# FFN down products of a two-layer trunk: 18 of 22 inner tiles in Strassen blocks, low parts made by VectorE

## The reference

```python
D_MODEL = 1024
D_FF = 2816
def swiglu(h, w_gu, w_down):
    g, u = jnp.split(h @ w_gu, 2, axis=-1)
    return (jax.nn.silu(g) * u) @ w_down
# x = x + gate * swiglu(modulate(rmsnorm(x), ...), w_gu, w_down)
```

## Time and profile before

| | us |
|---|---|
| runs | 2856.87, 2859.77, 2854.50 (median 2856.87) |
| profiled execution | 2856.11, of it span 2854.2 |
| TensorE, VectorE, ScalarE, GpSimd busy | 2752.9, 1492.7, 935.1, 1160.0 |
| mean granted clock of TensorE | 0.988 of 2.4 GHz |

### The profile page before, as it was taken

One profiled execution on the slowest core, in us unless ns is written; L12 is line 12 of the kernel. 1 busy time (PEld: TensorE's weight loads), 2 busy tenths in 40 slices (PEclk: granted clock), 3 DMA queues, 4 the chain that ended last, 5 costly groups with the idle time before them and its releaser, 6 DMA issues.

```text
span 2854.2 us, 61199 instructions
## 1 busy us (share of the span) xinstructions
PE 2752.9 (96%) x22137; PEld 2550.0 (89%) x22137; DVE 1492.7 (52%) x2891; ACT 935.1 (33%) x2091; POOL 1160.0 (41%) x1256
## 2 busy tenths in 40 slices
PE   6999999999999999999889999999999999999999
PEld 5898999998999999999787787878789999998998
DVE  4767678665333343423556666666676434335224
ACT  5121212355433443000543233332464444440004
POOL 4000000355555564333754333333376666653324
PEclk8999999999999999999999999999999999999999
DMA  7422111544555535631133524343453333246422
GB/s 260 135 75 92 51 39 38 196 132 135 190 195 191 186 103 196 222 113 43 56 114 102 159 86 148 97 136 109 151 181 117 112 95 118 89 131 244 150 67 82
DMA packets 335403, 366.41 MB, mean 128 GB/s; under 512 B 25188, under 2 KB 272087, under 8 KB 333799
## 3 DMA queue, kind: packets, MB, share of 16 engines
q1 hardware_dynamic: 311282, 327.13, 35.0%
q10 hardware_dynamic: 15732, 28.31, 2.8%
q0 software_dynamic: 8192, 8.40, 1.1%
HBM read 281.95 MB, written 81.82 MB: 127 GB/s over the span
## 4 chain that ended last, share of the span: by engine, by line
PE 87%; DVE 5%; ACT 3%; issue 2%; DMA 1%; POOL 1%; SPq 1%; DVEq 0%; ACTq 0%; POOLq 0%
PE bank L3630 23%; PE bank L3631 22%; PE bank L3632 22%; PE bank L4248 2%; PE bank L4367 2%; PE bank L4269 2%; PE bank L3759 1%; PE bank L4290 1%; PE bank L3921 1%; PE bank L3893 1%; PE bank L4355 1%; DVE xT L2475 1%; PE bank L3938 1%; DMA adae<-in_w_ada 1%; PE bank L4237 1%
## 5 line engine op out<-in xcount | busy, mean ns | idle before, releaser
L3630 PE MATMUL bank<-t_high,op_h 128*128 128x258 f32 x1736 | 496.8, 286 | 8.1 <-DVE t_low L3058 2.8
L3631 PE MATMUL bank<-t_low,op_h 128*128 128x258 f32 x1736 | 492.7, 284 | 0.0
L3632 PE MATMUL bank<-t_high,op_l 128*128 128x258 f32 x1736 | 490.4, 282 | 0.0
L3630 PE MATMUL bank<-hh,whi 128*128 128x344 f32 (+3 forms) x1324 | 439.2, 332 | 29.6 <-DVE ql L3246 7.2
L1271 POOL TENSOR_TENSOR op_l<-raw,op_h 128x512 fp32r<-128x512 f32 x252 | 347.1, 1378 | 282.9 <-ACT op_h L1937 270.9
L3632 PE MATMUL bank<-hh,wlo 128*128 128x344 f32 (+3 forms) x1324 | 422.6, 319 | 0.0
L3631 PE MATMUL bank<-hl,whi 128*128 128x344 f32 (+3 forms) x1324 | 422.2, 319 | 0.0
L3630 PE MATMUL bank<-down_high,whi 128*128 128x344 f32 x1056 | 341.0, 323 | 15.4 <-DVE xT L2475 9.7
L3630 PEld LDWEIGHTS bank<-t_high,op_h 128*128 128x128 f32 x1736 | 328.7, 189 | 21.3 <-issue 16.6
L3631 PE MATMUL bank<-down_low,whi 128*128 128x344 f32 x1056 | 338.0, 320 | 0.0
L3632 PE MATMUL bank<-down_high,wlo 128*128 128x344 f32 x1056 | 337.1, 319 | 0.0
(11 more groups left out here) (496 smaller groups left out, 5816.7 us busy)
## 6 DMA issues: line engine op xcount, KB each, us to landing
raw<-in_w_gu SPq DMA_DIRECT2D x84, 512.0 KB, 4.6
pk<-in_cache_ckv SPq DMA_DIRECT2D x256, 128.0 KB, 2.4
ada_x<-in_w_ada SPq DMA_DIRECT2D x28, 1024.0 KB, 7.1
down_high<-act_high SPq DMA_DIRECT2D x44, 516.0 KB, 5.8
down_low<-act_low SPq DMA_DIRECT2D x44, 516.0 KB, 6.5
act_high<-st_h SPq DMA_DIRECT2D x82, 258.0 KB, 5.0
act_low<-st_l SPq DMA_DIRECT2D x82, 258.0 KB, 5.4
wst<-in_w_in_even SPq DMA_DIRECT2D x28, 512.0 KB
```

The lines of the kernel that those rows point to most:

```text
L3630: mm(out, wh_, xh_, start=start, stop=False, skip_group_check=more)
L3631: mm(out, wh_, xl_, start=False, stop=False, skip_group_check=more)
L3632: return mm(out, wl_, xh_, start=False, stop=stop, skip_group_check=more)
```

## The change

In both layers 18 of the 22 tiles (all but 18 to 21 in layer 0; 1 to 18 in layer 1) are multiplied in blocks: three blocks of 6 tiles, DK = 3 tiles in each half, and in each block four units, one for each pair of output tiles, from the last pair to the first. A unit is seven products of two column halves, 3 tiles x 3 passes each: 126 matmuls of 258 columns. The last four tiles are multiplied as before (LAST_TILES).

- The operand of P1, P2 and P3 is taken from act_high and act_low in DRAM (`block_in`, rows of 258 words). The sums of the activation for P5, P7, P6, P4 are made in place by VectorE (`block_sum`) from a plain copy of the activation, which the gate/up units now store as well (`store_raw`, to act_raw) and SyncE loads again (`stage_load`): block 0 into rows 0 to 5 of xT, later blocks into a spare part of the operand regions. Their highs are made by ScalarE (`block_high`) and their lows by VectorE (`block_low`).
- xT's rows come back only after block 0's lows were made: rows 6 and 7 once the last activations are saved, then 3 to 5, then 0 to 2, all issued by SyncE.
- Weights of the down units go through the machinery of the gate/up units (`raw_load`, `weight_sum`, `op_high`, `op_low`).
- The results are added to xT piece by piece: P1, P1+P6 and P1+P6+P7 are copied out of the bank scaled by the gate (ScalarE, `scaled`) and added by VectorE; P2, P5, P4 and P3 are added from their banks with scale. The sample columns gather in csum.
- The counters of the semaphores and some places in SBUF are moved accordingly.

```diff
-DOWN_CHUNKS = [(0, 2), (2, 4), (6, 6), (12, 6), (18, 4)]
+DK = 3
+DOWN_BLOCKS = 3
+DOWN_UNITS = DOWN_BLOCKS * KT // 2
+LAST_TILES = ([18, 19, 20, 21], [19, 20, 21, 0])
...
+def down_order(t):
+    return (P5, P6, P4, P7) if t.l == 1 and t.u == 0 else (P5, P6, P7, P4)
+def down_after(t, p):
+    return {P1: P5, P2: P6, P5: P7, P6: P4, P7: P3, P4: P4, P3: P3}[p] if t.l == 1 and t.u == 0 else p
...
         # SyncE
+                for u in range(DOWN_UNITS):
+                    t = Unit(l, u, None, True)
+                    more = u < DOWN_UNITS - 2
+                    if u == 0:
+                        for q in range(2):
+                            sp.wait_ge(*a_saved[q](32 * (FT * l + 2 * DK)))
+                        block_in(t, P1)
+                        block_in(t, P2)
+                        sp.wait_ge(*td_in[1](DOWN_DMA * down_turn(t) + 32))
+                        block_in(t, P3)
+                    if more:
+                        sp.wait_ge(*op_lo(t.count(7, 7)))
+                        raw_load(l, t.next(2))
+                    if u == 0:
+                        for q in range(2):
+                            store(Unit(l, n - 1), q)
+                        for q in range(2):
+                            sp.wait_ge(*a_saved[q](32 * (FT * l + n)))
+                        sp.dma_start(xT[:, 2 * DK:KT, 0:T], x_rest[:, 2 * DK:KT, 0:T]).then_inc(x_in[1].sem, 16)
+                        sp.wait_ge(*x_in[1](32 * l + 16))
+                        sp.wait_ge(*td_lo(down_low(t, P7, 1)))
+                        sp.dma_start(xT[:, DK:2 * DK, 0:T], x_rest[:, DK:2 * DK, 0:T]).then_inc(x_in[1].sem, 16)
+                        sp.wait_ge(*td_dve(down_low(t, P4, 1)))
+                        sp.dma_start(xT[:, 0:DK, 0:T], x_rest[:, 0:DK, 0:T]).then_inc(x_in[0].sem, 16)
+                    if t.starts() and t.block() < DOWN_BLOCKS - 1:
+                        sp.wait_ge(*td_in[1](DOWN_DMA * down_turn(t) + DOWN_DMA))
+                        sp.wait_ge(*td_lo(down_low(t, P7, 1)))
+                        sp.wait_ge(*td_dve(down_low(t, P4, 1)))
+                        sp.wait_ge(*block_done[P3](t.count(2, 0)))
+                        stage_load(Unit(l, u + KT // 2, None, True))
+                    if t.ends() and t.block() < DOWN_BLOCKS - 1:
+                        after = t.next(1)
+                        block_in(after, P1)
+                        block_in(after, P2)
+                        sp.wait_ge(*td_in[1](DOWN_DMA * down_turn(after) + 32))
+                        block_in(after, P3)
...
         # ScalarE, end of the gate/up units and first down unit
+                act_high_half(0, 1, last)
+                gate2(0, last)
+                for p in down_order(after)[1:3]:
+                    block_high(after, p)
+                if l == 0:
+                    block_high(after, P4)
+                op_high(P3, after)
+                for u in range(DOWN_UNITS):
...
+                    if u == 0:
+                        gate2(1, last)
+                    p1_part(0, t)
+                    if u == 0:
+                        act_high_half(1, 0, last)
+                    p1_part(1, t)
+                    if u == 0:
+                        act_high_half(1, 1, last)
+                        if l == 1:
+                            block_high(t, P7)
...
         # VectorE
+                for u in range(DOWN_UNITS):
+                    t = Unit(l, u, None, True)
+                    more = u < DOWN_UNITS - 1
+                    sums = {1: (P5, P7), 2: (P6, P4)}.get(u % (KT // 2)) if t.block() < DOWN_BLOCKS - 1 else None
+                    source = Unit(l, (t.block() + 1) * (KT // 2), None, True)
+                    if u == 0:
+                        g2(1, last)
+                        a2(0, last)
+                        weight_sum(P5, t.next(1))
+                        a2(1, last)
+                        weight_sum(P7, t.next(1))
+                        block_low(t, P6)
+                        weight_sum(P6, t.next(1))
+                        block_low(t, P7)
+                        block_low(t, P4)
+                        weight_sum(P3, t.next(1))
+                        order.wait()
+                    else:
+                        p3_add(1, t.next(-1))
+                        if more:
+                            weight_sum(P5, t.next(1))
+                            weight_sum(P7, t.next(1))
+                    if t.block() == 0:
+                        if u < 2:
+                            dve.wait_ge(*x_in[1](32 * l + 16 * u + 16))
+                        elif u == 2:
+                            dve.wait_ge(*x_in[0](16 * l + 16))
+                    if u == 0:
+                        p5_add(0, t)
+                        p5_add(1, t)
+                    p1_add(0, t)
+                    p1_add(1, t)
+                    if t.starts() and u > 0:
+                        block_low(t, P7)
+                        block_low(t, P4)
+                    if more and u > 0:
+                        weight_sum(P6, t.next(1))
+                    p2_add(0, t)
+                    p2_add(1, t)
+                    if sums:
+                        block_sum(source, sums[0])
+                    if more and u > 0:
+                        weight_sum(P3, t.next(1))
+                    if u > 0:
+                        p5_add(0, t)
+                        p5_add(1, t)
+                    u2_add(0, t)
+                    u2_add(1, t)
+                    if sums:
+                        block_sum(source, sums[1])
+                    u3_add(0, t)
+                    u3_add(1, t)
+                    p4_add(0, t)
+                    p4_add(1, t)
+                    if t.ends() and more:
+                        block_low(t.next(1), P5)
+                        block_low(t.next(1), P6)
+                    p3_add(0, t)
...
         # TensorE
+                for u in range(DOWN_UNITS):
+                    t = Unit(l, u, None, True)
+                    for p in range(7):
+                        for q in range(2):
+                            if t.starts():
+                                if p in (P1, P2):
+                                    pe.wait_ge(*td_in[0](DOWN_DMA * down_turn(t) + DOWN_DMA))
+                                elif p == P3:
+                                    pe.wait_ge(*td_in[1](DOWN_DMA * down_turn(t) + DOWN_DMA))
+                                else:
+                                    pe.wait_ge(*(td_dve if p in (P6, P4) else td_lo)(down_low(t, p, q)))
+                            product(p, q, t)
```

525 lines of the change are left out of this document (348 added, 177 removed).

## The result

The changed kernel takes 2877.9 us (median of 5 runs, 2872.7 to 2880.8) against 2856.9 us: ratio 1.0080, 95% interval 1.0061 to 1.0099. It is slower by 0.8%, where 0.6% faster had been forecast, and lies above the range. Run once more beside the experiments it came to 2876.5 us, ratio 1.0068 (1.0051 to 1.0085). Medians and ratios leave out two executions in a slower state of the chip, one of the kernel with narrow GpSimd and one of that with idle matmuls.

A forecast was written before the change was run, and what follows sets the result against it. TensorE, busy 96% of the span, was taken as the bound: 2856.1 - 41.9 - 13.2 + 27.5 + 4.4 + 2.0 + 3.4 = 2838.3, so 2838 us, 0.6% faster; range 2821 to 2860.

The forecast's parts named there:

- Matmuls, -41.9: Down products: 2592 matmuls of 155.0 ns removed, 3024 of 119.0 ns added, minus 41.9 us.
- rival (d): The 258-column matmuls on the new tiles don't keep 119 ns; at 132 ns, 2877 us; chance 0.04.
- Old start gaps, -13.2: TensorE's waits at the start of the old down products, 6.8 and 6.4 us, go: minus 13.2 us.
- Start of the down products, +27.5: First down units wait for low parts, adds and staging: 14.7 us in layer 0, 12.8 in layer 1.
- Between blocks, +4.4: Loads of the next block's P1 and P2 operands come 1.1 us late, four times; 15 us at 250 GB/s.
- Last four tiles, +2: Their 4.2 MB load after the last unit's P1 and P2 costs 2 us for both layers (8 at 300).
- Prices of the side work: Durations per operation in the down units; VectorE's work in a block takes 47.8 of 60 us, so it fits.
- rival (c): VectorE becomes the bound in every block, some 20 us: 2858 us, no change; chance 0.14.
- Costed at nothing, the extra stores: Storing every gated product once more, 528 KB per unit, goes beside a DMA share of 0.32 at no cost.
- Clock, +3.4: Granted clock falls after stalls at the start of the down products, one per layer counted: 3.4 us (0 to 10).
- rival (b): DMA decides: the queue runs at 290 instead of 350 to 400 GB/s, about 2866 us; chance 0.17.
- The signs named in the prediction: Forecast wrong if a unit lasts over 15.3 us, the clock falls over four times in the stage, or gate/up lengthens.

The follow-up runs named there:

- narrow GpSimd: Changed kernel, but GpSimd makes only 8 of 128 columns of the low parts of the down units' weights; 2851.4 us, ratio 0.9987.
- idle matmuls: Changed kernel with 12 idle 128-column products ahead of P3 of units 0 and 1 and P1 of units 1 and 2, both layers; 2872.4 us, ratio 1.0055.
- all moves and the PSUM hand-over: Changed kernel with five reorderings of gate, loads, stores and sums, plus P1 and U2 handed to VectorE through PSUM; 2836.2 us, ratio 0.9943.
- the second look: The changed kernel unaltered, run and profiled once more beside the experiments; 2876.5 us, ratio 1.0068.
- the moves: Changed kernel with gate order at the start, cut staging read, earlier store, block 0's sums one unit later and last tiles read early; 2840.8 us, ratio 0.9955.
- all moves, narrow GpSimd: Changed kernel with the five reorderings, and GpSimd making only 8 of 128 columns of the down weights' low parts; 2813.6 us, ratio 0.9860.

## Why the prediction was wrong, step by step

**Matmuls, -41.9**: right in kind, slightly too small. In a full unit of the changed kernel 126 matmuls follow each other in 15.1 us between waits, 0.120 each, so rival (d) is out. The counts 336 and 129 include matmuls that only reach into the window; from start to start the spacings before are 119.9 and 157.4 ns, and the same sum gives 45. With all moves and the PSUM hand-over TensorE's busy time in the down stages is 19.7 and 20.0 us below before, for 20.95, at a mean granted clock of 0.98: that it agrees with 41.9 is in part luck.

**Old start gaps, -13.2**: right. Of the waits for `xT L2475` (9.7 us, 20 times) only the six of 0.3 us at the last four tiles are left, now under line 2687 (2.0 us).

**Start of the down products, +27.5**: right in kind and order, somewhat too large. The chain P6 low, P7 low, `p5_add`, `p4_add`, staging is all there: 2.9, 0.7, 0.5, 3.4, 2.6 and 1.1 us in layer 0, 11.1 in sum for 14.7, and 8.6 for 12.8 in layer 1. The single sizes are off: 2.9 us for P6's low where 1.1 had been put, 0.5 at the first `p5_add` for 4.3, 3.4 at `p4_add` for 2.4. `block_sum` sat idle for 6.2 us until the staging had landed, as foreseen. Unit 2 still began 48.1 us after unit 0, where the forecast has 44.7, because the matmuls behind the waits ran slower (a clock of 0.76 to 0.97 in the windows of 10 us there).

**Between blocks, +4.4**: 0.9, 0.9, 0.6 and 0.7 us, 3.2 in all. The number is near by luck: three of the four waits are for `block_low` on VectorE and only one is for the load that the sum had in mind. With narrow GpSimd, where VectorE is in time, all four are for that load, and there they are 0.6, 0.8, 2.2 and 1.5 us, 5.1 in sum. (Its bound "15 at 250 GB/s" should be 20 by its own rule. The estimate beside it from the Trainium skill ("DMA: Bandwidth & Descriptors", section "How a descriptor splits into AXI transactions"), some 15% more beats, comes to 11% by the same counts, 36.5 beats for 33 as a mean over the starts; no run isolates it.) **Last four tiles, +2**: 7.2 us, the transfer being later than worked out, and a slow stretch behind it (0.66 for ten us).

**Prices of the side work**: the step that failed. I wrote that VectorE's block of four units has 47.8 of 60 us, with one price per operation whatever GpSimd does, and turned rival (c) away by "0.57 us for 344-column adds with GpSimd busy, no spread in it". That row reads `xT<-bank,mod,xT`: one of its inputs is in PSUM. Nearly all that the change adds to VectorE (block sums, low parts, adds of P1, U2 and U3) has both inputs in SBUF. The kernel before already showed what those cost, a few rows below the ones that I quoted:

```profile
1106.60 1.28 POOL L1271 TENSOR_TENSOR op_l<-raw,op_h 128x512 fp32r<-128x512 f32 x1 [0.95 <-ACT op_h L1937]
...
1106.87 1.29 DVE L2993 TENSOR_TENSOR tq<-tq,u 128x258 f32<-128x258 f32 x1 [0.27 <-ACT tq L1975]
```

The same operation stands in the earlier trace rows with 0.42 us, at a moment when GpSimd was idle. Between 700 and 900 us it took 0.42 us all nine times that it began with GpSimd idle and 1.53 all nine times that GpSimd was running. Its neighbour `tq<-tq,bank` (line 2987), which has one input in PSUM, took 0.42 us all eighteen times, nine of them begun while GpSimd ran: the kernel before held the whole comparison. In the gate/up units of before it cost nothing, since VectorE was busy for 17.3 of 40 us; in the changed down units VectorE had a few us to spare in 15 and lost 4.2 (3.4 and 0.8, above). TensorE waited 1.2 us ahead of each of six such units, and 1.7 and 0.5 us at two places behind each change of block: 15.7 us in both layers that the sum did not have. With narrow GpSimd all of these waits are gone. The Trainium skill says it in "SBUF — State Buffer", section "Who interferes with whom": a VectorE instruction with two inputs in SBUF contends with a GpSimd instruction that reads SBUF, and whichever issues second stands until the first is done, while one with a single SBUF input does not contend (outside certain fast modes, which the page names). The trace agrees with this rule in all three points (1.24, 1.39 and 0.47 us above); I had not weighed it.

Rival (c) thus was the true case for the down stages, with the right place and nearly the right size (some 20 us; the narrowing gave 23 to 27), and had 0.14. Its time, 2858, was missed by 20 us as well, since the extra stores, the last tiles and the clock came on top.

**Costed at nothing, the extra stores**: the second miss. I looked at the DMA share (0.32) and not at the place in SyncE's queue: the store stands behind loads of up to 3.17 MB and ScalarE, then TensorE wait for it. I had named that wait and said that TensorE wants the copy 7 us later; the store took longer than that. Without the wait for the first down operand it was 13 us in the first profile and 8 in the second.

**Clock, +3.4**: it fell more often than the term allowed for. It fell in five of the 10 us windows of block 0 and after the three longest waits in gate/up (0.50 to 0.57 in the 2 to 2.5 us behind them); after that of 1.15 us near 2569 it stayed at 1.00. TensorE's own account of the down stages splits the missing 24 us in two halves: it waits 32.6 us more than before where 20.7 had been forecast, and its busy time fell by 26.3 us for 41.9, 12 us more than the 3.4 put down for the clock (in the second look 14 and 8). That is an account and not a cause. In block 0 most of it ran beside waits that would have come anyway (idle matmuls: between nothing and 7 us in layer 0, 3 in layer 1); after the waits of gate/up and of the last tiles, where TensorE is the bound, it came on top.

What cannot be settled by these runs: how the 24 us of the down stages divide between the turns, the last tiles and the clock to better than a few us, since they cover one another; and rival (b), the rate of the queue as such, was never tested alone. Against it speaks that the moves took 32 to 36 us away without a change in bytes, that the queue moved 414 GB/s in the window 1160 to 1170 us above, and that the staging for block 1 had landed by 39.8 us after the last gate/up product, for 37 in the forecast.

The signs named in the prediction came out: a unit lasted over 15.3 us, the clock fell more than four times, gate/up lengthened.

## What to carry to other kernels

Price a VectorE operation by where its inputs are and by what GpSimd does at that moment: with both in SBUF, take the duration beside a running GpSimd operation, and look in the trace for the pair of durations of one line. Before a small store is given a free ride, read what stands ahead of it in its queue and which engine's buffer it holds. The idea itself was sound: with the loads and sums moved, the same matmuls give 0.5% less than the kernel before.

## What the runs showed of the hardware

GpSimd pays as well: in the rows above its 384-wide operation takes 1.01 us alone and 1.39 to 1.41 when it starts during a VectorE operation with both inputs in SBUF; one of 24 elements (all moves, narrow GpSimd) grew from 0.26 to 0.59 and 0.86 us. Moving one input to PSUM takes an operation out of this (0.41 beside GpSimd for 1.13) at no price in its own time.

In this kernel idle matmuls held the granted clock at 1.00 through a stretch of waits, but in block 0 this changed the stages by only -3.3 and +2.1 us. Where TensorE waits for nothing else it pays to avoid the wait: without the 3.7 and 3.5 us before the last tiles the down stages were 7.3 and 6.6 us shorter (4.5 and 6.9 against the second look).
